# Cross attention's output projection and the feed forward layer in one block, with the norm's root applied behind the projections

## What is computed

```python
def rms_norm(x, g):
    xf = x.astype(jnp.float32)
    y = xf * lax.rsqrt(jnp.mean(xf * xf, axis=-1, keepdims=True) + EPS)
    return (y * g.astype(jnp.float32)).astype(x.dtype)

h = h + xo.reshape(b, s, XA_HEADS * XA_HEAD_DIM) @ xa_w_o[l]        # 512 -> 1024

fn = rms_norm(h, norm_ffn[l])
g = fn @ ffn_w_gate[l]                                              # 1024 -> 2816
g_pad = jnp.pad(g, ((0, 0), (CONV_W - 1, 0), (0, 0)))
g_conv = ffn_conv_b[l] + sum(cw[i] * g_pad[:, i:i + s] for i in range(CONV_W))
h = h + (jax.nn.silu(g_conv) * (fn @ ffn_w_up[l])) @ ffn_w_down[l]  # 2816 -> 1024
```

## Time and profile before

| | |
|---|---|
| median of 3 runs | 3494.46 us (3489.35 to 3498.19) |
| profiled execution, its own time | 3493.44 us |
| its span, first to last instruction | 3491.7 us |
| mean granted TensorE clock | 0.953 |
| TensorE matmul busy | 3156.6 us, 90% |
| VectorE, ScalarE, GpSimd busy | 1757.9, 978.6, 836.1 us |
| the stage of this change | 848.20 to 1686.75 us |

### The profile page before, as it was taken

One profiled execution on the slowest core, in us unless ns is written; L12 is line 12 of the kernel. 1 busy time (PEld: TensorE's weight loads), 2 busy tenths in 40 slices (PEclk: granted clock), 3 DMA queues, 4 the chain that ended last, 5 costly groups with the idle time before them and its releaser, 6 DMA issues. The chain is left out here.

```text
span 3491.7 us, 38580 instructions
## 1 busy us (share of the span) xinstructions
PE 3156.6 (90%) x15262; PEld 2493.5 (71%) x15262; DVE 1757.9 (50%) x2675; ACT 978.6 (28%) x1839; POOL 836.1 (24%) x500
## 2 busy tenths in 40 slices
PE   5999988888899999999899999997798999999869
PEld 3777777666687787787678787875576777777647
DVE  4234566534532132233476868786343357777751
ACT  2332344314321010011233233332131244444430
POOL 1221000341332233332233333332122221111002
PEclk8998999999899999999899999999899999999889
DMA  2112000110111111112211111111222100000011
GB/s 103 37 36 88 13 1 13 37 49 29 44 48 44 47 48 42 49 47 72 66 43 49 61 46 63 43 67 55 115 91 84 37 31 31 25 31 25 7 61 72
DMA packets 45274, 170.26 MB, mean 49 GB/s; under 512 B 5040, under 2 KB 5312, under 8 KB 43968
## 3 DMA queue, kind: packets, MB, share of 16 engines
q1 hardware_dynamic: 44832, 161.85, 13.6%
q0 software_dynamic: 288, 6.29, 0.4%
HBM read 145.06 MB, written 23.07 MB: 48 GB/s over the span
## 5 line engine op out<-in xcount | busy, mean ns | idle before, releaser
L176 PE MATMUL acc<-x_hi,w_hi 128*128 128x512 f32 x2064 | 859.6, 416 | 88.5 <-DVE x_lo L267 43.3
L169 POOL CAST w_hi<-w_raw 128x1024 fp32r<-128x1024 f32 x217 | 237.0, 1092 | 2519.3 <-PE acc L178 1464.4
L177 PE MATMUL acc<-x_lo,w_hi 128*128 128x512 f32 x2064 | 831.5, 403 | 0.0
L178 PE MATMUL acc<-x_hi,w_lo 128*128 128x512 f32 x2064 | 829.8, 402 | 0.0
L171 POOL TENSOR_TENSOR w_lo<-w_raw,w_hi 128x1024 fp32r<-128x1024 f32 x217 | 544.3, 2508 | 17.4
L176 PEld LDWEIGHTS acc<-x_hi,w_hi 128*128 128x128 f32 x2064 | 396.8, 192 | 211.1 <-issue 81.0
L178 PEld LDWEIGHTS acc<-x_hi,w_lo 128*128 128x128 f32 x2064 | 397.6, 193 | 97.8
L177 PEld LDWEIGHTS acc<-x_lo,w_hi 128*128 128x128 f32 x2064 | 398.9, 193 | 87.2 <-issue 1.2
L2225 DVE SCALAR_TENSOR_TENSOR acc<-ev_upad,cols,acc 128x1024 f32<-128x1024 f32 x232 | 298.1, 1285 | 4.2
L378 DVE TENSOR_TENSOR h<-h,acc 128x1024 f32 (+1 forms) x40 | 48.9, 1221 | 317.1 <-PE acc L178 317.1
L176 PE MATMUL aux<-x_hi,w_hi 128*128 128x512 f32 x448 | 191.9, 428 | 0.0
(11 more groups left out here) (491 smaller groups left out, 5068.5 us busy)
## 6 DMA issues: line engine op xcount, KB each, us to landing
w_raw<-in_stream SPq DMA_DIRECT2D x217, 512.0 KB, 3.4
h<-in_x SPq DMA_DIRECT2D x16, 512.0 KB, 8.7
spill_h<-h SPq DMA_DIRECT2D x8, 512.0 KB, 5.3
spill<-ev_zst SPq DMA_DIRECT2D x8, 512.0 KB, 3.1
h_even<-spill_h SPq DMA_DIRECT2D x8, 512.0 KB, 7.8
ev_zr<-spill SPq DMA_DIRECT2D x8, 512.0 KB, 3.5
spill_h<-h_even SPq DMA_DIRECT2D x8, 512.0 KB, 5.3
h<-spill_h SPq DMA_DIRECT2D x8, 512.0 KB, 6.5
```

What stands on the lines that cost most here:

```text
L169: pool.tensor_copy(k.w_hi[slot][:], k.w_raw[slot][:]).then_inc(k.w_split, 1)
L176: pe.matmul(out, w_hi, x_hi, start=start, stop=False)
L177: pe.matmul(out, w_hi, x_lo, start=False, stop=False)
L178: return pe.matmul(out, w_lo, x_hi, start=False, stop=stop)
```

## The change

One block, `block_ffn`, does the output projection and all of the feed forward layer.

- The input of gate and up tiles is h times the gain only (`LateNorm`): ScalarE copies with the gain as scale, VectorE subtracts in one operation, both tile by tile while the output projection still runs. Since the root is one number per token (a column), it is multiplied on the projected tiles: VectorE reads the gate from `acc` and multiplies it by `root` (in place of ScalarE's copy), and multiplies silu times up by `root` once more.
- `late_tile` is used for the first gate tile and the first down tile of each part. It does all contraction steps but the last for both halves, and then the last step for both; it waits for each step's low part.
- The sum over partitions (`on_tensor`) stands behind the first gate tile.
- `g_hi`, `g_lo` and the input trade places in SBUF, `gate`, `conv` and the sums share space as before, and the buffer `prod` is gone.
- The block's semaphores are its own and are cleared at its end.

```diff
+class LateNorm:
+    def high(self, act, j):
+        act.activation(self.x_hi[:, j, :], self.k.h[:, j, :], ACT.Copy, scale=self.gain_of(j)).then_inc(self.hi, 1)
+    def low(self, dve, j):
+        dve.wait_ge(self.hi, j + 1)
+        dve.scalar_tensor_tensor(self.x_lo[:, j, :], self.k.h[:, j, :], self.gain_of(j), self.x_hi[:, j, :].bitcast(F32),
+                                 ALU.mult, ALU.subtract).then_inc(self.lo, 1)
+    def on_tensor(self, pe):
+        pe.wait_ge(self.early.summed, KD - 1)
+        for c in (0, HALF):
+            mm = pe.matmul(self.total_in[:, c:c + HALF], self.k.ones, self.early.acc[:, c:c + HALF], start=True, stop=True)
+        mm.then_inc(self.total, 1)
+    def root_of(self, act):
+        act.wait_ge(self.total, 1)
+        act.activation(self.rstd, self.total_in[:, 0:SEQ], ACT.Ln, scale=1.0 / D, bias=self.k.eps[:, 0:1]).then_inc(self.root, 1)
+        act.wait_ge(self.root, 1)
+        act.activation(self.rstd, self.rstd, ACT.Exp, scale=-0.5).then_inc(self.root, 1)
...
+        @block.sync
+        def _(sp):
+            stream_loads(k, sp, wa + 2, da[LAST] + 2)
+            for j in range(KD + 2):
+                if j < KD:
+                    stream_loads(k, sp, da[LAST] + 2 + j, da[LAST] + 3 + j)
+                if j >= 2:
+                    sp.wait_ge(summed, base + (1 + LAST) * KD + j - 1)
+                    sp.dma_start(k.spill_h[:, j - 2, :], k.h[:, j - 2, :]).then_inc(k.h_spilled, 16)
+        @block.gpsimd
+        def _(pool):
+            stream_splits(k, pool, wa + 1, end + 1)
+        @block.tensor
+        def _(pe):
...
+            def late_tile(n, x_hi, x_lo, kt, lo, count):
+                slot = n % 2
+                pe.wait_ge(k.w_split, n * 2 + 2)
+                pe.wait_ge(k.acc_free[slot], n // 2)
+                for qs in (range(kt - 1), range(kt - 1, kt)):
+                    for c in (0, HALF):
+                        for q in qs:
+                            if c == 0:
+                                pe.wait_ge(lo, count + q + 1)
+                            mm = product3(pe, acc[:, slot, c:c + HALF], k.w_hi[slot][:, q * P:(q + 1) * P],
+                                          k.w_lo[slot][:, q * P:(q + 1) * P], x_hi[:, q, c:c + HALF], x_lo[:, q, c:c + HALF],
+                                          q == 0, q == kt - 1)
+                mm.then_inc(k.lin_done, 1)
+            over_tiles(pe, wa, wb, tile(o_hi, o_lo, XA_HEADS))
+            for p, tiles in enumerate(FFN_PARTS):
+                if p == 0:
+                    late_tile(ga[p], x_hi, x_lo, KD, late.lo, 0)
+                    late.on_tensor(pe)
+                    over_tiles(pe, ga[p] + 1, da[p], tile(x_hi, x_lo, KD))
+                else:
+                    over_tiles(pe, ga[p], da[p], tile(x_hi, x_lo, KD))
+                late_tile(da[p], g_hi, g_lo, tiles, s["lo"], first[p])
+                over_tiles(pe, da[p] + 1, da[p] + KD, tile(g_hi, g_lo, tiles))
+        @block.scalar
+        def _(act):
+            load_log_exp(act)
+            for j in range(KD):
+                act.wait_ge(summed, base + j + 1)
+                late.high(act, j)
+                squares.square(act, j, k.h[:, j, :])
+            late.root_of(act)
...
+                with act.Fori(0, tiles) as i:
+                    act.wait_ge(s["conved"], i + (first[p] + 1))
+                    act.activation(conv[:], conv[:], ACT.Silu).then_inc(s["silued"], 1)
+                    act.wait_ge(s["producted"], i + (first[p] + 1))
+                    settle(k, act)
+                    act.activation(g_hi[:, i, :], conv[:], ACT.Copy).then_inc(s["hi"], 1)
...
+        @block.vector
...
+            for j in range(KD):
+                add(wa + j, j)
+                if j:
+                    late.low(dve, j - 1)
+                    squares.add(dve, j - 1)
+            late.low(dve, KD - 1)
+            squares.add(dve, KD - 1)
+            late.wait_root(dve)
...
+                    dve.wait_ge(k.lin_done, i * 2 + (a + 1))
+                    dve.tensor_tensor(gate[:, 2:SEQ + 2], acc[:, slot, :], root[:], ALU.mult).then_inc(k.acc_free[slot], 1)
+                    dve.wait_ge(k.acc_free[slot], i + (a // 2 + 1))
...
+                    dve.tensor_tensor(conv[:], conv[:], acc[:, other, :], ALU.mult).then_inc(k.acc_free[other], 1)
+                    dve.wait_ge(k.acc_free[other], i + ((a + 1) // 2 + 1))
+                    dve.tensor_tensor(conv[:], conv[:], root[:], ALU.mult).then_inc(s["producted"], 1)
+                    dve.wait_ge(s["hi"], i + (first[p] + 1))
+                    dve.tensor_tensor(g_lo[:, i, :], conv[:], g_hi[:, i, :].bitcast(F32), ALU.subtract).then_inc(s["lo"], 1)
...
+    k.release()
...
         block_cross(k)
-        k.squares = EarlySquares(k, "ffn")
-        block_residual(k, "xa_o", k.x_hi, k.x_lo, XA_HEADS, squares=k.squares)
...
-        for part, tiles in enumerate(FFN_PARTS):
-            k.g_hi, k.g_lo = at(f"g{part}_hi", 64, [P, tiles, SEQ], F32R), at(f"g{part}_lo", 96, [P, tiles, SEQ], F32R)
-            block_ffn_in(k, part)
...
-            block_residual(k, f"ffn_down{part}", k.g_hi, k.g_lo, tiles, squares=k.squares if last else None,
-                           spill=k.spill_h if last else None)
+        block_ffn(k)
```

More of the change, by code:

```diff
@@ L1541, in block_cross, with __init__, gain_of, wait_root @@
     k.release()
[L1544 to L1558, removed]
+class LateNorm:
+    def __init__(self, k, name, gain, x_hi, x_lo, early, rstd, total_in):
+        self.k, self.gain, self.x_hi, self.x_lo, self.early, self.rstd, self.total_in = k, gain, x_hi, x_lo, early, rstd, total_in
+        self.hi, self.lo, self.total, self.root = (k.own(f"{name}_{s}") for s in ("hi", "lo", "total", "root"))
+    def gain_of(self, j):
+        return self.k.cols[:, self.gain + j:self.gain + j + 1]
+    def high(self, act, j):
[14 more added lines that the diff above has]
+        act.activation(self.rstd, self.rstd, ACT.Exp, scale=-0.5).then_inc(self.root, 1)
+    def wait_root(self, eng):
+        eng.wait_ge(self.root, 2)
@@ new lines, in block_ffn @@
+def block_ffn(k):
+    wa, wb = STREAM["xa_o"]
+    ga = [STREAM[f"ffn_gu{p}"][0] for p in range(len(FFN_PARTS))]
+    da = [STREAM[f"ffn_down{p}"][0] for p in range(len(FFN_PARTS))]
+    end = STREAM[f"ffn_down{len(FFN_PARTS) - 1}"][1]
+    first = [sum(FFN_PARTS[:p]) for p in range(len(FFN_PARTS))]
+    LAST = len(FFN_PARTS) - 1
+    o_hi, o_lo = k.x_hi, k.x_lo
+    x_hi, x_lo = k.at("x3_hi", 64, [P, KD, SEQ], F32R), k.at("x3_lo", 96, [P, KD, SEQ], F32R)
+    g_hi, g_lo = k.at("g_hi", 0, [P, FFN_PARTS[0], SEQ], F32R), k.at("g_lo", 32, [P, FFN_PARTS[0], SEQ], F32R)
+    squares = EarlySquares(k, "ffn")
+    gate = k.at("ffn_gate", 128, [P, SEQ + 2])
+    conv = k.at("ffn_conv", 132.25, [P, SEQ])
+    root = k.at("ffn_root", 136.25, [P, SEQ])
+    late = LateNorm(k, "fn", COLS["norm_ffn"], x_hi, x_lo, squares, root[:], k.aux)
+    k.squares = EarlySquares(k, "even")
+    reloaded, stored, summed = k.residual_sems
+    base, k.residuals = k.residuals * KD, k.residuals + 1 + len(FFN_PARTS)
+    names = "padded conved chain silued producted hi lo".split()
+    s = {n: k.own(f"ffn_{n}") for n in names}
+    acc = k.acc
@@ L1561, in _ @@
         def _(sp):
-            stream_loads(k, sp, a + 2, b + 2)
+            stream_loads(k, sp, wa + 2, da[LAST] + 2)
[5 more added lines that the diff above has]
+                    sp.dma_start(k.spill_h[:, j - 2, :], k.h[:, j - 2, :]).then_inc(k.h_spilled, 16)
         @block.gpsimd
         def _(pool):
-            stream_splits(k, pool, a + 1 if a else 0, min(b + 1, N_STREAM))
+            stream_splits(k, pool, wa + 1, end + 1)
@@ L1568, in _, with tile @@
         @block.tensor
         def _(pe):
[L1570 to L1576, removed]
+            def tile(x_hi, x_lo, kt):
+                return lambda n, slot, turn: linear_tile(k, pe, n, slot, turn, x_hi, x_lo, kt)
@@ new lines, in _ @@
+            for j in range(KD):
[3 more added lines that the diff above has]
+            late.root_of(act)
+            act.wait_ge(s["padded"], 1)
+            for p, tiles in enumerate(FFN_PARTS):
+                with act.Fori(0, tiles) as i:
[4 more added lines that the diff above has]
+                    act.activation(g_hi[:, i, :], conv[:], ACT.Copy).then_inc(s["hi"], 1)
@@ L1593, in _ @@
+            for j in range(KD):
+                act.wait_ge(summed, base + (1 + LAST) * KD + j + 1)
+                k.squares.square(act, j, k.h[:, j, :])
         @block.vector
         def _(dve):
-            if norm is not None:
-                norm.on_vector(dve)
-            step = Steps(dve, s["chain"], 2 * first_tile)
-            dve.memset(gate[:, 0:2], 0.0).then_inc(s["padded"], 1)
[L1599 to L1615, removed]
@@ new lines, in add @@
+            def add(n, done):
+                dve.wait_ge(k.lin_done, n + 1)
+                h = k.h[:, done % KD, :]
```

(9 more changed lines are left out.)

22 lines of the change are left out of this document (18 added, 4 removed).

## The result

The changed kernel takes 3440.84 us (median of 4 runs, 3437.36 to 3452.12), the kernel before 3491.9 us beside it (4 runs). The ratio is 0.9854, with a 95% interval of 0.9828 to 0.9880. In two later comparisons it was 0.9865 (0.9838 to 0.9892) and 0.9871 (0.9848 to 0.9894), with medians of 3445.98 and 3446.66 us. In each of these one execution of the kernel before was far longer than the others (6252.49 and 3655.77 us) and is left out. The forecast, 3445.0 in place of 3494.46, is a ratio of 0.9858.

What follows compares the result with a forecast made beforehand. Holes in TensorE's sequence, busy 90% of the span, bound the kernel. Stage terms 784.0 + 1.6 + 1.0 + 0.2 + 1.7 = 788.5 us, with 0.5 for clearing 49.5 less, gave a median of 3445.0 us, range 3439 to 3456.

Steps and rivals of the forecast that it cites:

- The loss to be had: The stage from output projection to feed forward layer takes 838.55 us against 784.0 of bare matmuls: 54.55 us lost.
- The five seams: Block ends between up, down and gate tiles, without a norm: 26.0 us of idling and slow starts fall to zero.
- U: End of a part's last up tile on TensorE; g_lo's subtraction was forecast to end 7.6 us after it.
- (b): Rival: a seam keeps its idle time because a wait held for satisfied is not; about 3470 us, chance 0.06.
- The seam with the norm: Output projection to first gate tile: 26.9 us lost shrink to a 1.0 us stall and 0.2 for a slow start.
- The sum over partitions: The norm's sum behind the first gate tile waits for nothing and takes 1.7 us; the root after it costs zero.
- The loops: Within gate and up pairs, VectorE's added work does not reach TensorE: zero, with cover of 2.7 and 3.6 us.
- The end: At the new block's end, clearing its semaphores costs 0.5 us more.
- The sum: Stage 788.5 us in place of 838.55, 50.0 less; with the clearing 49.5 less; median 3445.0 us.
- (a): Rival: covers too short, x_lo or g_lo late at the norm's seam and parts 1 and 2; 3453 us, chance 0.14.
- (c): Rival: TensorE's clock falls to 1.2 GHz during 788 us without idling; with a fifth low about 3538 us, chance 0.03.

## Why the prediction was right, step by step

- **The loss to be had.** 784.0 us of bare work held: the longest stretch has 3118 matmuls in 727.5 us, 0.2333 each.
- **The five seams.** Forecast zero, found zero: no wait at any of them. The chain's steps were forecast to end at U+5.0, U+6.2, U+7.6 and ended at U+4.9, U+6.1, U+7.5. The two added products show the 0.7 us of slack at parts 1 and 2 to be real: it is now 0.9. Putting the barriers back costs 30.2 us, not 26.0, since the late norm makes the chain of these seams longer. So the two halves of the change are worth more together than apart: the one block with the old norm gives 838.55 - 813.30 = 25.25 us, the late norm with the barriers 838.55 - 818.44 = 20.1, both 50.3. The 26 us that I used for rival (b) were right only for the kernel before.
- **The seam with the norm.** Stall forecast 1.0 with 0.2 for a slow start, found 0.64 and 0.27, 0.91 together (a gap of 0.80 in excess of a matmul's turn, then 0.11). The mis-sized part: GpSimd's subtraction ended 3.86 us behind the projection's end (889.97), not 4.0, and x_lo of step 6 at 894.92, which is 4.95, not 5.1. The prediction's own terms, 5.1 less 4.2, give 0.9 and were rounded up. The cause is shown twice, by GpSimd's shortened subtraction and by the other order in VectorE's queue; each takes the stall away. What the late last step is worth at this gate tile was not tried.
- **The sum over partitions.** 1.7 forecast, 1.72 found, at the full clock and without a wait. TensorE never waited for the root.
- **The loops.** Nothing reached TensorE, even with two products more per pair.
- **The end.** 0.5 forecast, 0.6 found.
- **The sum.** 784.0 + 1.65 + 0.91 + 1.72 = 788.28, measured 788.25, forecast 788.5. The span fell by 49.9 us: 50.3 in the stage, 4.7 in front of it, minus 5.1 behind it, of which 0.6 is the clearing. That the forecast 49.5 and the 49.9 lie so near is partly luck: the 4.7 us in front of the stage is no part of the change and moves by up to 12 us from one execution to another, and of the 5.1 us behind it only 0.6 was forecast (0.5). The stage is where the prediction was right on its merits.
- **The rivals.** (a) did not come at this kernel's lengths; its mechanism, g_lo too late, is what the usual order of the down tiles brings (803.7 us). (b) is out, since none of the waits that it named is there. (c) is out: the clock is 1.00 over the 727.76 us without an idle moment. That one core does not trip a limiter is also what the Trainium skill states (TensorE: Matmul & The Clock Gate, Part 1), and the trace agrees.

## What to carry over

When a block's end stands between a producer's last step and a consumer, count what the consumer can do without that step: here 36 to 42 matmuls (8.4 to 9.8 us) covered a chain of 7.5 us, but only with the last contraction step of both halves put off. Size such a chain with the neighbour that shuts it out in place, here GpSimd's subtraction: an operation of 1.3 us took 3.2 and one of 1.2 us took 3.4. And what is linear in a norm can be brought forward, so that TensorE comes to the sum at its full clock and never waits for the root. Of that gain of 25 us, 10 came from the place of the sum.

## What the runs showed of the hardware that I had not expected

TensorE's clock makes the executions differ, and in a stage that the change doesn't touch. In the first model's attention the granted clock of 500 to 620 us was 0.99 in one execution of the changed kernel and 0.93 in another, with the same program:

```profile
500.00:620.00 120.00, 104.27 (x748) 87.29 (x747) 72.12 (x158) 52.97 (x125) 0.00 (x0) 0.99 0.03 10
...
500.00:620.00 120.00, 105.72 (x716) 88.61 (x714) 68.13 (x153) 50.81 (x125) 0.00 (x0) 0.93 0.03 10
...
578.00:612.00 34.00, 29.70 (x205) 24.74 (x204) 14.96 (x31) 15.50 (x39) 0.00 (x0) 0.95 0.09 32
...
578.00:612.00 34.00, 30.98 (x172) 26.15 (x172) 12.49 (x27) 13.23 (x33) 0.00 (x0) 0.75 0.08 31
```

The first and third rows are of the execution that reached the stage at 843.53, the others of the one at 852.64. Compared matmul by matmul, the second falls behind by 6.0 us between 578 and 612 us, and by 3.3 between 426 and 485, where its clock was 0.94 instead of 1.00. The profiled execution of the kernel before lost time only in the earlier of these stretches (0.91) and began the stage in between, at 848.20. Of the eleven profiles of the changed kernel and its variants, six began the stage between 843.5 and 844.5 us and five between 852.6 and 855.6. What decides between the two was not tried.

Slow starts did not follow the length of the idle time alone. Beyond the idle time itself TensorE lost 0.27 us behind 0.64 us (the changed kernel) and 1.46 us (two more products), a handover with no slow matmul. Behind 2.05 us it lost 1.8 once and 0.26 once (barriers back), behind 2.47 us 1.8, behind 3.17 us 3.0 and 1.8 (usual order), behind 5.85 us between 1.6 and 3.0 (barriers back). Nor are the matmuls behind a pause always slow at once: at the beginning of the stage of the changed kernel the first ones have the full rate of 0.23 us from start to start, and those from 844.56 to 847.96 take 0.42.

```profile
844.09 0.40 PE L178 MATMUL acc<-x_hi,w_lo 128*128 128x512 f32 x1
844.33 0.42 PE L176 MATMUL acc<-x_hi,w_hi 128*128 128x512 f32 x1
...
845.40 0.63 PE L176 MATMUL acc<-x_hi,w_hi 128*128 128x512 f32 x1
845.83 0.63 PE L177 MATMUL acc<-x_lo,w_hi 128*128 128x512 f32 x1
...
847.96 0.40 PE L176 MATMUL acc<-x_hi,w_hi 128*128 128x512 f32 x1
848.20 0.39 PE L177 MATMUL acc<-x_lo,w_hi 128*128 128x512 f32 x1
```
